# Search junk in free columns, ones in pieces, four gathers moved behind the first gates, five up blocks loaded earlier, Pool waiting for the row sums

## The reference

```python
def peer(h, w_q, sub_keys, w_down, w_up):
    q = (ht @ w_q).reshape(T, 8, 2, 128)
    scores = einsum('thic,hikc->thik', q, sub_keys)        # 128 keys in each half
    sv, si = top_k(scores, 16)
    cand = sv[:, :, 0, :, None] + sv[:, :, 1, None, :]
    best, ci = top_k(cand.reshape(T, 8, 256), 16)
    expert = i1 * 128 + i2                                  # 16384 experts, 128 picks a token
    gate = softmax(best)
    hid = gelu(einsum('cd,ckd->ck', x, w_down[expert]))
    out = einsum('ck,ckd->cd', gate * hid, w_up[expert])
```

## Time and profile before

| | |
|---|---|
| median of 3 runs | 1535.36 us (1534.59 to 1537.02) |
| the profiled execution: its own time | 1542.12 us |
| the profiled execution: its span | 1540.3 us |
| TensorE matmul busy | 1493.3 us, 97% |
| VectorE, ScalarE, GpSimd busy | 58%, 31%, 47% |
| HBM read | 519.48 MB, 338 GB/s over the span |
| granted TensorE clock, mean | 0.993 |

### The profile page before, as it was taken

How to read it: one execution, slowest core, us unless ns; L and a number is a source line. 1 busy time by engine, 2 the same in 40 slices (tenths; PEclk the granted TensorE clock), 3 DMA queues, 4 the chain that set the end, 5 groups by cost and what they waited for, 6 DMA issues and landing times.

```text
span 1540.3 us, 29722 instructions
## 1 busy us (share of the span) xinstructions
PE 1493.3 (97%) x10668; PEld 1449.4 (94%) x10668; DVE 887.1 (58%) x2900; ACT 476.6 (31%) x1199; POOL 721.3 (47%) x632
## 2 busy tenths in 40 slices
PE   7999999999999999999999999989999999999996
PEld 5789999999999999999977899989999999999996
DVE  1631889856886344443723339998388843444473
ACT  4663331227882000000046542211588600000001
POOL 5568023338996223323457741333599832233250
PEclk9999999999999999999999999999999999999999
DMA  7344899998999999999944468999999999999993
GB/s 276 131 137 165 282 357 406 408 402 314 382 387 392 409 409 410 409 410 410 384 164 161 155 217 301 407 403 409 350 374 378 384 409 409 410 409 410 410 409 135
DMA packets 144992, 523.12 MB, mean 340 GB/s; under 512 B 17008, under 2 KB 17264, under 8 KB 144496
## 3 DMA queue, kind: packets, MB, share of 16 engines
q1 hardware_dynamic: 67696, 240.62, 41.6%
q0 software_dynamic: 55296, 201.35, 33.4%
q10 hardware_dynamic: 21888, 79.70, 13.0%
HBM read 519.48 MB, written 1.05 MB: 338 GB/s over the span
## 4 chain that ended last, share of the span: by engine, by line
PE 78%; DVE 8%; DMA 7%; ACT 3%; issue 2%; POOL 1%; SPq 0%; another core or an unknown queue 0%; DVEq 0%; POOLq 0%; ACTq 0%
PE ps L937 77%; DMA arena<-in_rows,ret 4%; DVE arena L1554 2%; DMA spare<-in_wu 1%; DVE arena L1501 1%; DMA raw<-in_wd 1%; DVE oh_buf L1469 1%; POOL w_lo L551 1%; DVE oh_buf L1466 1%; DVE arena L1473 1%; ACT arena L626 1%; DMA raw<-in_wm 1%; PE ps L945 1%; ACT hT_hi L653 1%; ACT w_hi L638 1%
## 5 line engine op out<-in xcount | busy, mean ns | idle before, releaser
L937 PE MATMUL ps<-arena,raw 128*128 128x160 f32 (+1 forms) x2944 | 416.7, 301 | 4.6 <-DMA raw<-in_wd 4.4
L937 PE MATMUL ps<-arena,w_raw 128*128 128x160 f32 (+1 forms) x2944 | 414.9, 299 | 2.8 <-issue 2.8
L937 PEld LDWEIGHTS ps<-arena,raw 128*128 128x128 f32 x2944 | 407.1, 192 | 6.3 <-DMA raw<-in_wd 4.6
L937 PEld LDWEIGHTS ps<-arena,w_raw 128*128 128x128 f32 x2944 | 403.5, 190 | 4.6 <-issue 4.5
L568 POOL DMA_INDIRECT arena<-in_wu,ret x192 | 190.7, 993 | 362.8 <-DVE oh_buf L1618 272.2
L568 POOL DMA_INDIRECT arena<-in_rows,ret x192 | 202.7, 1056 | 298.3 <-ACT ret L826 104.5
L1618 DVE SCALAR_TENSOR_TENSOR oh_buf<-arena,ret,oh_buf 128x1024 f32<-128x1024 f32 x126 | 161.8, 1284 | 239.1 <-DMA arena<-in_wu,ret 238.9
L551 POOL TENSOR_TENSOR w_lo<-raw,w_hi 128x1024 fp32r<-128x1024 f32 x80 | 193.3, 2424 | 100.7 <-PE ps L937 67.9
L1501 DVE SCALAR_TENSOR_TENSOR arena<-arena,ps 128x1024 f32<-128x1024 f32 x128 | 153.7, 1213 | 0.0
L916 ACT ACTIVATE arena<-ident 128x768 f32<-128x768 f32 x2 | 1.7, 842 | 448.4 <-PE ps L937 448.4
L584 POOL TENSOR_SCALAR oh_buf<-iota,ret 128x128 f32<-128x128 f32 x160 | 127.2, 803 | 15.4 <-PE ps L937 11.3
(11 more groups left out here) (144 smaller groups left out, 1779.4 us busy)
## 6 DMA issues: line engine op xcount, KB each, us to landing
raw<-in_wd SPq DMA_DIRECT2D x108, 512.0 KB
w_raw<-in_wd SPq DMA_DIRECT2D x108, 512.0 KB
raw<-in_wm SPq DMA_DIRECT2D x80, 512.0 KB
raw<-in_wu ACTq DMA_DIRECT2D x28, 512.0 KB
raw<-in_wu SPq DMA_DIRECT2D x28, 512.0 KB
w_raw<-in_wu SPq DMA_DIRECT2D x28, 512.0 KB
w_raw<-in_wu ACTq DMA_DIRECT2D x28, 512.0 KB
low_rows<-in_wu SPq DMA_DIRECT2D x22, 512.0 KB
```

What stands on the lines that cost most here:

```text
L937: return nc.tensor.matmul(out, lhsT, rhs, start=start, stop=stop, skip_group_check=shared)
```

## The change

- **Junk.** `found` moves from columns between the scores and the candidates to 14 x 54 columns at the arena's end, which nothing uses at that time. It has 14 places rather than 24, so VectorE waits at every seventh lookup (that the eighth before it is done) rather than at every eighth.
- **Ones.** Since the junk is gone from there, more columns are free while the second half is searched. The ones are written in 12 pieces at blocks 34 to 45 and 6 pieces at blocks 55 to 60; the large piece at block 77 is gone.
- **Gathers.** Pool asks for 45 gathers rather than 49 ahead of the first `build_first`, and between two builds for at most two.
- **Up blocks.** SyncE issues the five early up loads ahead of down block 8 rather than ahead of down block 16.
- **Row sums.** In layer 1, Pool's first `low_part` waits until all row sums of layer 0 are made.

```diff
-ONES_FROM, ROWS_AT, ONES = 12, 8, 432
+ONES_FROM, ROWS_AT, ONES = 34, 8, 434
...
-SC_AT = (RING_AT, RING_AT - HALVES * KEYS - (24 + RH) * CAND)
-EQ_AT = SC_AT[1] + HALVES * KEYS
-CD_AT = EQ_AT + 24 * CAND
+SC_AT = (RING_AT, RING_AT - HALVES * KEYS - RH * CAND)
+CD_AT = SC_AT[1] + HALVES * KEYS
 HT_AT = RING_AT + RING * DM
+FOUND, EQ_AT = 14, HT_AT + DC * DENSE
...
-                blocks(sp, load_down_again, DOWN_RAW, UP_EARLY_AT, DOWN_RAW)
                 for j in range(UP_EARLY):
                     load_up(j, j)
-                blocks(sp, load_down_again, UP_EARLY_AT, MORE_GATES_AT, DOWN_RAW)
+                blocks(sp, load_down_again, DOWN_RAW, MORE_GATES_AT, DOWN_RAW)
...
                 def low_part(b, s, first=False):
                     n = b + l * LAYER
+                    if b == 0 and l:
+                        pool.wait_ge(row_used, l * GATHERS)
...
-                asked = EARLY + RING - 1
+                asked = EARLY + IN_FLIGHT
                 for q in range(asked):
                     gather(q)
                 pool.wait_ge(ids_split, l + 1)
                 for g in range(TGROUPS):
                     build_first(g)
                     if g > 2:
-                        free = min(ROWS, dots_after(g + G_FROM - 2) + RING - 1)
+                        free = min(ROWS, dots_after(g + G_FROM - 2) + RING - 1, asked + 2)
                         for q in range(asked, free):
                             gather(q)
                         asked = max(asked, free)
...
-                    if ONES_FROM + RAW <= b < ONES_FROM + RAW + ONES_PIECES:
-                        write_ones(b - ONES_FROM - RAW)
+                    if ONES_FROM <= b < ONES_FROM + ONES_PIECES:
+                        write_ones(b - ONES_FROM)
+                    if EXP_AT[1] < b <= EXP_AT[1] + LAST_PIECES:
+                        write_ones(ONES_PIECES + b - EXP_AT[1] - 1)
...
-                    if b == IDS_AT:
-                        act.wait_ge(idg_done, TILES * (l + 1))
-                        late = BLOCKS * DENSE - SC_AT[1]
-                        nc.scalar.activation(arena[:, SC_AT[1]:BLOCKS * DENSE], ident[:, 0:1].to_broadcast([P, late]),
-                                             ACT.Copy, scale=0.0, bias=1.0).then_inc(ones_done, 1)
...
-                        if j > 2:
-                            dve.wait_ge(dve_step, eights[j - 3])
                         h = j // 4 + j // 2 % 2 * (RH // 2)
                         for k in range(8):
-                            n = h * TOPK + j % 2 * 8 + k
-                            step(nc.vector.scalar_tensor_tensor(found[:, (j * 8 + k) % 24, :], places,
+                            n, i = h * TOPK + j % 2 * 8 + k, j * 8 + k
+                            if i >= FOUND and i % (FOUND // 2) == 0:
+                                dve.wait_ge(dve_step, looked[i - FOUND // 2 - 1])
+                            step(nc.vector.scalar_tensor_tensor(found[:, i % FOUND, :], places,
```

More of the change, by code:

```diff
@@ L138 @@
 UP_BANKS = ((0, 1, 2), (3, 4), (5, 6), (7,))
-UP_EARLY, UP_EARLY_AT = 5, 2 * DOWN_RAW
+UP_EARLY = 5
 TURN_QK, SCORE_BEFORE = 11, (12, 14)
@@ L171 @@
 UPT_FREE_AT = 103
-assert HT_AT + DC * DENSE <= BLOCKS * SEQ and UPT_AT + DC * SEQ <= UPT_FREE_AT * DENSE and UPT_AT + DC * SEQ <= PROJ_AT
+assert EQ_AT + FOUND * CAND <= BLOCKS * SEQ and UPT_AT + DC * SEQ <= UPT_FREE_AT * DENSE and UPT_AT + DC * SEQ <= PROJ_AT
 assert CD_AT + RH * CAND <= RING_AT and G_FROM * DENSE <= SC_AT[1]
 assert BS_AT + GROUPS <= SMALL_FREE_AT * DENSE and GF_AT + DM <= GF_FREE_AT * DENSE
-ONES_PIECES = -(-(SC_AT[1] - G_FROM * DENSE) // ONES)
-assert ONES_FROM + RAW + ONES_PIECES < IDS_AT
+ONES_PIECES, LAST_PIECES = -(-(SC_AT[1] - G_FROM * DENSE) // ONES), -(-(RING_AT - SC_AT[1]) // ONES)
+assert ONES_FROM + ONES_PIECES <= EXP_AT[1] and EXP_AT[1] + LAST_PIECES < IDS_AT
 IDX_AT, HID_AT, GATE_AT = 768, 864, 960
@@ L321, in build_trunk @@
         first_id = ps[:, 5, P:2 * P].rearrange("p (h k) -> p h k", h=RH)
-        found = at(EQ_AT, 24, CAND)
+        found = at(EQ_AT, FOUND, CAND)
         def block_of(b):
@@ L814, in write_ones @@
                         act.wait_ge(more_rows_sb, 16 * PARTS * (l + 1))
-                    first = G_FROM * DENSE + i * ONES
-                    size = min(first + ONES, SC_AT[1]) - first
+                    if i < ONES_PIECES:
+                        first, end = G_FROM * DENSE + i * ONES, SC_AT[1]
+                    else:
+                        first, end = SC_AT[1] + (i - ONES_PIECES) * ONES, RING_AT
+                    size = min(first + ONES, end) - first
                     nc.scalar.activation(arena[:, first:first + size],
@@ L1546, in _ @@
                                             ALU.subtract).then_inc(best_done, 1)
-                    eights = []
+                    looked = []
                     for j in range(2 * RH):
-                        if j > 2:
-                            dve.wait_ge(dve_step, eights[j - 3])
                         h = j // 4 + j // 2 % 2 * (RH // 2)
                         for k in range(8):
-                            n = h * TOPK + j % 2 * 8 + k
-                            step(nc.vector.scalar_tensor_tensor(found[:, (j * 8 + k) % 24, :], places,
+                            n, i = h * TOPK + j % 2 * 8 + k, j * 8 + k
+                            if i >= FOUND and i % (FOUND // 2) == 0:
+                                dve.wait_ge(dve_step, looked[i - FOUND // 2 - 1])
+                            step(nc.vector.scalar_tensor_tensor(found[:, i % FOUND, :], places,
                                                                 cif[:, t, n:n + 1], pay[:, h, :], ALU.is_equal,
                                                                 ALU.mult, accum_out=idf[:, t, n:n + 1]))
-                        eights.append(steps[0])
+                            looked.append(steps[0])
                         if t == 0 and j % 4 == 3:
@@ L1623, in _ @@
                 dve.wait_ge(h_done, (l + 1) * G_FROM)
-                dve.wait_ge(ones_done, (l + 1) * (ONES_PIECES + 1))
+                dve.wait_ge(ones_done, (l + 1) * (ONES_PIECES + LAST_PIECES))
                 gate(0, 0)
```

## The result

| | before | changed |
|---|---|---|
| median of 20 runs | 1538.61 us (1534.59 to 1541.67) | 1544.55 us (1538.99 to 1547.92) |
| ratio | | 1.0035, 95% interval 1.0026 to 1.0045 |
| the profiled execution: own time, span | 1542.12, 1540.3 us | 1546.25, 1544.5 us |

The change makes the kernel slower, by 0.35% or 5.4 us (the two medians themselves lie 5.9 us apart). The forecast was 1537.0 us with a range of 1530 to 1542, and the measured time lies outside it. The gain forecast for layer 0 is not there; the cost forecast for the gathers is there in both layers, at the size given. The three runs of before on which the forecast stood (1535.36) also lay 3.3 us under the median of twenty. All ratios in this document are of runs in the fast state; the only run in the other state, one of the twelve of e5, took 3322.20 us.

The account below looks back on a forecast made before the run. TensorE's matmuls are busy 1493.3 of 1540.3 us, so only its waits and lower clock can move the time. Layer 0 -1.14 and layer 1 +2.76 give +1.6 us on 1535.36: 1537.0 us, range 1530 to 1542.

Parts of the forecast that it names:

- The 3.90 us go: Layer 0, group 0's gates: with four gathers fewer ahead, TensorE's 2.17 us wait and 1.73 us slow first group vanish.
- Rival 1: Layer 0's first gates: unprofiled runs may lack the wait, so no gain and 5.5 us cost, 1540.9 us; chance 0.2.
- rival 2: Layer 1, down block 40: the stall and low clock behind it go, 7.3 us faster, 1529.7 us; chance 0.15.
- rival 4: Layer 0 gets layer 1's stall at down block 40, at most 7.3 us slower, 1544.3 us; chance 0.1.
- Gathers in the loop: Pool's queue behind builds 3 to 7: four more gathers use up its lead, TensorE waits 2.76 us more in each layer.
- Up blocks 0: Five up loads issued earlier: their DMA backlog is gone before the gathers either way, so 0 us.
- ones and junk 0: Ones in pieces on ScalarE, and junk moved with lookup waits seven back: 0 us each; ones bounded at 0.5 a layer.
- row sums 0: Layer 0's end: Pool's low parts wait for VectorE's sums; up to 5.2 us if TensorE waited, but hidden, so 0.
- rival 3: Pool keeps up: gathers put into groups 3 to 5 fill only idle time, cost 0, 1531.5 us; chance 0.1.

Follow-up runs that it names:

- e5: The changed kernel with the gathers alone put back (49 ahead of the first build, loop limit as before); ratio 0.9991 against the kernel before.
- e2: The kernel before with only the five early up loads moved ahead of down block 8; ratio 1.0003, median 1535.87 us.
- e1: The kernel before with the change of the gathers alone (45 ahead, at most two between builds); ratio 1.0034, median 1540.18 us.
- e6: The kernel before with gathers 45 to 48 put behind build 1, no limit of two; ratio 0.9988, median 1537.34 us.
- e7: The kernel before with 43 gathers ahead of the builds instead of 49, and the limit of two; ratio 1.0058, median 1547.46 us.
- e9: The changed kernel with gathers 45 to 48 behind build 1 and the limit of two removed; ratio 0.9985 against the kernel before, median 1537.17 us.
- e8: The kernel before with ScalarE issuing the odd down blocks from block 24 rather than 40 (two load queues); ratio 1.0005, median 1539.05 us.
- e10: The kernel before with gathers 45 to 48 behind build 1 and two down rows fewer ahead of the gates; ratio 1.0009, median 1541.20 us.

## Why the prediction was wrong

The forecast was -3.90 + 2.76 in layer 0 and +2.76 in layer 1.

- **The step that failed: "The 3.90 us go."** The row was right, and the wait did go. But it was booked in full, as if every execution had it. The profiles of before and of e2 to e5, all with 49 gathers ahead, show a wait at group 0 in two of ten layers: the one given (2.17 us, 3.90 with the slow first group) and layer 1 of e2 (1.76 us, 1.83 with its first group). That is a mean of 1.1 us an execution over both layers, by my estimate, where the sum had 3.90. Rival 1 named the failure and priced it right: 2 x 2.76 = 5.5 us, measured 5.4. It should have had the largest chance.
- **What the four gathers give back at the gates is little.** The first gates of layer 0 start at 347.59 to 349.60 in the five profiles with 49 gathers ahead, and at 347.07 to 348.50 in the five with 43 or 45 (the changed kernel, e1, e6, e7, e9). These ranges overlap. Ahead of the gates TensorE loses time in several places, and from 160 us to group 0 of layer 0 its idle time sums to 3.9 to 5.9 us in all eleven kernels with one load queue, whether group 0 waits or not. The prediction priced the stall at block 40 at 7.3 us as if it stood on the path alone (rivals 2 and 4). e8 took it away in both layers, and the median did not move.
- **Gathers in the loop, +2.76 us a layer: right.** Measured 123.16 - 120.45 = 2.71 in layer 1, with build 8 at 1124.70 for 1125.19 forecast, nine late groups for "some nine", and Pool idle last at build 3. e7 extends the account by two gathers to 125.70 in layer 0.
- **Up blocks 0, ones and junk 0, row sums 0: right**, with 1.0003, 1.0001 and 1.0010 each alone and 0.9991 together. The row at TensorE decided that the wait for the row sums is worth nothing, and it is. The lines themselves were misread: two low parts of 4.68 us can't run beside sums of 15.43. They ran beside the first sum alone, 5.71 us for the usual 1.28. So the price of that overlap was 5.71 - 1.28 = 4.4 us and not 5.2. The Trainium skill, SBUF — State Buffer, "Who interferes with whom", calls the shared ports an exclusive lock, and one sum held while its seven followers run at their usual pace agrees with that.
- **Rivals.** 1 happened. 2 did not (stall of 3.24 us at block 40 still there in layer 1). 3 did not: Pool lost its lead. 4 happened in form, since layer 0 shows the stall, but so do e2 to e6, whose times are those of before, so it is no effect of the change.
- **The base.** The forecast stood on three runs at 1535.36. With rival 1's 5.5 us on the 1538.61 of twenty runs it would have been 1544.1.

What stays open: what decides whether an execution waits at block 40, at block 77 or at group 0. The places don't simply stand in for each other: layer 1 of e2 waits at block 40 and at group 0, and layer 1 of e10 at none of the three. Whether e6 and e9 are faster than before, by the 2 us that their ratios say, is not settled by their intervals; the 1.1 us estimated above would be part of it.

## What to carry to other kernels

An instruction moved on a queue that runs in order costs its full time where that queue has no idle time, and nothing where the queue waits anyway: look for the bracket with idle time and put the work there. Four gathers behind builds 3 and 4 cost 2.7 us a layer, the same four behind build 1 nothing. Before a wait is booked as a gain, look for it in other executions: here it stood in two layers of ten, once in an execution slower than the median and once in a faster one. Ask also what else stands between it and the work that really sets the date: in e8, in a stretch where the DMA engines are full, a stall of over 3 us was removed in both layers and the median stayed. And a mean over merged rows can hide one long instruction: ask for the rows one by one before a rate is read from them.

## What was unexpected on the chip

- In the profile of before the DMA share is 1.03 at 403 to 409 GB/s from 220 to 320 us. In that stretch, loads on a second queue from block 24 on removed TensorE's stall (none in six layers, against 18 of 22 with one queue), and the median didn't move (1.0005). That the queues share out a fixed rate would fit this; no run shows the shares.
- A gather holds Pool's queue for 1.24 us (0.94 or 1.03 shown, 0.15 to 0.30 ahead of it), four fifths of a build of two one-hots (1.59).
- One VectorE sum of 128x1024, which started 0.07 us behind Pool's two low parts of the same shape, took 5.71 us for 1.28; the sums behind it took 1.39 each.
- The granted clock behind a wait of TensorE is not set by the wait's length alone. The 64 records behind the stall at block 40 took 8.96 us at full clock behind 3.36 us of wait (changed kernel, layer 0) and behind 3.51 (e2, layer 1), but 11.91 us behind 3.24 (changed kernel, layer 1, mean clock 0.76 in 1010 to 1020). Behind the 0.3 us waits of the late groups the clock stayed at 1.00, though their gates take 1.13 us for 1.05.
